# Mixture-of-experts loop with three resident weight sets, one extra block ahead of its loop, and four gather buffers

## The reference, cut to what matters

```python
D_MODEL, SEQ, CTX_LEN, N_EXPERTS, TOP_K, D_EXPERT = 1024, 256, 256, 32, 2, 512

# per layer, after the mixers
lg = h @ w_rg + b_rg                       # 4 groups, the best one is taken
le = (h @ w_re + b_re) of that group       # 8 experts, the best two are taken
weights = softmax(lg)[group] * top2_probabilities
for block in blocks_of_tokens_sorted_by_expert:
    ys = (silu(xb @ w_gate[e]) * (xb @ w_up[e])) @ w_down[e]
out = sum over the two experts of weight * ys      # back in token order
x = x + gate * out
...
return rms_norm(x, final_g)
```

## Time and profile before

| | us |
|---|---|
| median of 3 runs | 2103.83 (2101.32 to 2107.59) |
| the profiled execution, its own time | 2107.49 |
| its span, first to last instruction | 2105.7 |
| PE busy in it | 1875.1 (89%) |
| layer 0, first gate_up to the end of the last down | 637 to 1172 |
| layer 1, the same | 1565 to 2068 |

### The profile page before, as it was taken

How to read it: one execution, slowest core, us unless ns; L and a number is a source line. 1 busy time by engine, 2 the same in 40 slices (tenths; PEclk the granted TensorE clock), 3 DMA queues, 4 the chain that set the end, 5 groups by cost and what they waited for, 6 DMA issues and landing times.

```text
span 2105.7 us, 27927 instructions
## 1 busy us (share of the span) xinstructions
PE 1875.1 (89%) x9715; PEld 997.8 (47%) x9716; DVE 685.3 (33%) x1467; ACT 516.1 (25%) x1052; POOL 152.2 (7%) x190
## 2 busy tenths in 40 slices
PE   5799999999979999977999679989978989898985
PEld 2576666668743333322333367767943323232323
DVE  1456355445442111111111365574441111111112
ACT  2444444432231101100011254443220101110111
POOL 0035021000000000000000206130000000000000
PEclk8899999999989999988999799999989999999997
DMA  6446565223256999965999423233467989999992
GB/s 221 164 162 220 200 215 199 107 71 94 81 239 281 421 421 421 421 275 236 389 421 420 145 90 103 88 102 116 154 263 311 421 361 421 421 421 421 421 421 100
DMA packets 96042, 550.47 MB, mean 261 GB/s; under 512 B 14162, under 2 KB 15650, under 8 KB 42724
## 3 DMA queue, kind: packets, MB, share of 16 engines
q1 hardware_dynamic: 83108, 526.89, 63.1%
q0 software_dynamic: 4224, 11.35, 1.9%
q10 hardware_dynamic: 8640, 11.28, 1.5%
HBM read 537.15 MB, written 12.32 MB: 261 GB/s over the span
## 4 chain that ended last, share of the span: by engine, by line
PE 70%; DMA 12%; DVE 7%; ACT 5%; issue 3%; SPq 1%; ACTq 0%; DVEq 0%; POOL 0%; POOLq 0%
PE ps L724 17%; DMA moe<-in_w_exp_gate_up_dram 10%; PE ps L467 8%; PE ps L709 7%; PE ps L469 7%; PE ps L468 7%; PE ps L736 7%; PE ps L658 2%; PE ps L614 2%; PE ps L585 2%; PE ps L716 1%; PE ps L507 1%; PE ps L596 1%; DVE w_lo L1186 1%; PE ps L760 1%
## 5 line engine op out<-in xcount | busy, mean ns | idle before, releaser
L724 PE MATMUL ps<-moe,ht 128*64 128x512 f32 x2048 | 451.4, 593 | 22.8 <-DMA moe<-in_w_exp_gate_up_dram 22.8
L724 PEld LDWEIGHTS ps<-moe,ht 128*64 128x64 f32 x2048 | 150.2, 137 | 316.7 <-issue 291.6
L467 PE MATMUL ps<-ht_hi,w_hi 128*128 128x512 f32 (+1 forms) x736 | 268.6, 365 | 20.8 <-DVE ht_lo L1209 18.1
L468 PE MATMUL ps<-ht_lo,w_hi 128*128 128x512 f32 (+1 forms) x736 | 257.4, 350 | 0.0
L469 PE MATMUL ps<-ht_hi,w_lo 128*128 128x512 f32 (+1 forms) x736 | 257.3, 350 | 0.0
L1482 DVE TENSOR_TENSOR arena<-aux,ps 128x256 f32<-128x256 f32 x64 | 26.9, 421 | 687.9 <-ACT aux L1083 687.9
L736 PE MATMUL ps<-moe,arena 128*64 128x512 f32 x1024 | 231.4, 594 | 2.5 <-DVE arena L1503 2.5
L1186 DVE TENSOR_TENSOR w_lo<-ws,w_hi 128x1024 fp32r<-128x1024 f32 (+1 forms) x124 | 150.4, 1217 | 234.4 <-ACT w_hi L900 234.3
L709 PE MATMUL ps<-arena,ht 128*64 128x512 f32 x816 | 212.1, 630 | 4.7 <-DVE ht L1435 4.7
L467 PEld LDWEIGHTS ps<-ht_hi,w_hi 128*128 128x128 f32 x736 | 139.8, 190 | 70.9 <-issue 39.6
L900 ACT ACTIVATE w_hi<-ws 128x1024 fp32r<-128x1024 f32 (+1 forms) x124 | 127.4, 1027 | 187.5 <-PE ps L469 150.3
(11 more groups left out here) (220 smaller groups left out, 1984.6 us busy)
## 6 DMA issues: line engine op xcount, KB each, us to landing
moe<-in_w_exp_gate_up_dram SPq DMA_DIRECT2D x256, 1024.0 KB, 13.4
moe<-in_w_exp_down_dram SPq DMA_DIRECT2D x128, 1024.0 KB, 16.4
moe<-in_w_mod_dram SPq DMA_DIRECT2D x32, 1536.0 KB, 6.8
ws<-in_w_in_dram SPq DMA_DIRECT2D x92, 512.0 KB, 3.9
y_rows<-arena ACTq DMA_DIRECT2D x164, 64.0 KB, 5.6
ws<-in_w_branch_dram SPq DMA_DIRECT2D x16, 512.0 KB, 3.5
ws<-in_w_out_dram SPq DMA_DIRECT2D x16, 512.0 KB, 3.3
aux<-in_rpb_a_dram POOLq DMA_DIRECT2D x64, 64.0 KB, 3.1
```

The source lines that it names most:

```text
L467: pe.matmul(ps[:, bank, 0:cols], w[:, k, :], a_hi, start=(i == 0), stop=False)
L468: pe.matmul(ps[:, bank, 0:cols], w[:, k, :], a_lo, start=False, stop=False)
L724: mm = pe.matmul(ps[BLK * j:BLK * j + BLK, bank, :].rearrange("p (g n) -> p g n", g=2), x[:, at:at + BLK], w[:, k, 512 * j:512 * j + 512]. ...
```

## The change

It does three things in one edit.

1. **Three weight sets.** The third set lies in `ws` (24 KB, the slots of the mixers' weights), in `arena` (16 KB) and in `ht` (8 KB). For that, the routing scratch `r` moves from `arena` to `aux`, and the pairs of `xg`, `hid`, `hid_t`, `act_g`, `ysb`, of the PSUM banks of `gate_up` (2, 3) and `down` (4, 5), and the use of two `pick` buffers in the loop become one each. The loop has 10 passes of three bodies, and two experts follow behind it. SP asks for the weights of expert `e` when `turn_h`, then `down`, of expert `e - 3` are done; the last piece of the first third set waits for `hturn_done`, since it overwrites part of `ht`. SP waits at the end for `down` of expert 29, since the next layer's weights go into `ws`.
2. **The first extra block** stands outside the loop over extra blocks, which runs only if `n > BLK + MORE`.
3. **Four pairs of gather buffers**, so POOL's gathers wait for no tile.

```diff
-        xg = [part(ht_flat, 2 * i, 2) for i in range(2)]
-        hid = [part(arena, 34 + i, 1) for i in range(2)]
-        ysb = [part(arena, 40 + 2 * i, 2) for i in range(3)]
+        xg, xs = part(ht_flat, 0, 2), part(ht_flat, 2, 2)
+        hid, hid_t = part(arena, 34, 1), part(arena, 35, 1, 2, P)
+        ysb, ysb_o = part(arena, 40, 2), part(arena, 42, 1)
...
+        third = [part(ws_flat, 8 * i, 8, 2, D) for i in range(3)] + [part(arena, 24, 8, 2, D), part(arena, 16, 8, 2, D), part(ht_flat, 8, 8, 2, D)]
+        eights = [[part(moe, 48 * i + 8 * j, 8, 2, D) for j in range(6)] for i in range(2)] + [third]
...
+                load_expert(lambda w: w[l, 2], 2, range(5))
+                sp.wait_ge(g["hturn_done"].sem, g["hturn_done"].at(l, width(l) // P - 1, 1))
+                load_expert(lambda w: w[l, 2], 2, (5,))
...
+                    sp.wait_ge(g["hidt_done"].sem, NE * l + e - SLOTS + 1)
+                    load_expert(source, slot, range(4))
+                    sp.wait_ge(g["down_done"].sem, NE * l + e - SLOTS + 1)
+                    load_expert(source, slot, range(4, 6))
...
+                def expert(e, i, q):
+                    done, landed = NE * l + e, loads_before(l, q) + i + 1
+                    pe.wait_ge(g["xt_copied"].sem, xt0 + e + 1)
+                    pe.wait_ge(gu_in[q].sem, landed * 64)
+                    gate_up(2, xg, wgu[q])
...
+                    with pe.If(n > BLK):
+                        def more_block(b):
+                            more_slots(pe.snap(n_more, min_val=0, max_val=64), wgu[q], wd[q])
+                            pe.reg_add(n_more, n_more, 1)
+
+                        more_block(BLK // MORE)
+                        with pe.If(n > BLK + MORE):
+                            with pe.Fori(BLK // MORE + 1, w_all // MORE) as b:
+                                with pe.If(n > b * MORE):
+                                    more_block(b)
...
+                    pe.wait_ge(g["hidt_copied"].sem, done + 1)
+                    pe.wait_ge(g["y_copied"].sem, done + 1)
+                    down(4, hid_t, wd[q], g["down_done"].sem)
+
+                with pe.Fori(0, ROUNDS) as i:
+                    for q in range(SLOTS):
+                        expert(SLOTS * i + q, i, q)
+                for q in range(TAIL):
+                    expert(SLOTS * ROUNDS + q, ROUNDS, q)
...
-                    if tile >= 2:
-                        pool.wait_ge(g["comb"].sem, g["comb"].at(l, tile - 2))
```

More of the change, by code:

```diff
@@ L268, in hybrid_block, with loads_before @@
         bias_in = [g[f"bias{i}"] for i in range(4)]
[L269 to L273, removed]
+        gu_in, wd_in = [g[f"gu_in{i}"] for i in range(SLOTS)], [g[f"wd_in{i}"] for i in range(SLOTS)]
+        yg_got = [g[f"yg_got{i}"] for i in range(4)]
+        def loads_before(l, q):
+            return sum(len(range(q, NE, SLOTS)) for _ in range(l))
         def width(l):
@@ L781, in _ @@
                 pick_x(pick[1], range(nt))
[L782 to L790, removed]
-                        pe.nop(nofuse=True)
[L792 to L808, removed]
@@ L1068, in _ @@
                     act.reg_mov(n_more, 0)
[L1069 to L1071 removed]
+                    act.sem_inc(g["y_copied"].sem, 1)
+                    act.sem_inc(g["y_saved"].sem, 32)
                     act.sem_inc(g["yo_copied"].sem, 1)
@@ L1110, in _ @@
-                        with act.If(n > HALF):
-                            save_rows(ysb[s], act.snap(row + HALF, min_val=0, max_val=2 * NTOK), g["yt_saved"], first=HALF, rows=HALF)
-                            act.reg_add(n_tails, n_tails, 1)
-                        act.nop()
-                act.wait_ge(y_saved[0].sem, 32 * 16 * (l + 1) + 32)
-                act.wait_ge(y_saved[1].sem, 32 * 16 * (l + 1) + 32)
+                    act.nop()
+                    act.wait_ge(g["down_done"].sem, done + 1)
@@ new lines, in expert @@
+                    nc.scalar.activation(ysb, ps[:, 4, :], ACT.Copy).then_inc(g["y_copied"].sem, 1)
+                    act.wait_ge(g["y_copied"].sem, done + 2)
+                    act.wait_ge(g["yo_saved"].sem, act.snap(n_more, min_val=0, max_val=64) * 64 + 64)
+                    save_rows(ysb, row, g["y_saved"], rows=HALF)
+                    with act.If(n > HALF):
+                        save_rows(ysb, act.snap(row + HALF, min_val=0, max_val=2 * NTOK), g["yt_saved"], first=HALF, rows=HALF)
+                        act.reg_add(n_tails, n_tails, 1)
@@ L1116, in _ @@
+                    act.nop()
+                with act.Fori(0, ROUNDS) as i:
+                    for q in range(SLOTS):
+                        expert(SLOTS * i + q)
+                for q in range(TAIL):
+                    expert(SLOTS * ROUNDS + q)
+                act.wait_ge(g["y_saved"].sem, 32 * NE * (l + 1) + 32)
                 act.wait_ge(g["yt_saved"].sem, act.snap(n_tails, min_val=0, max_val=64) * 32 + 32)
@@ new lines, in expert @@
+                    dve.wait_ge(g["xt_done"].sem, xt0 + e + 2)
+                    copy_xg()
+                    dve.wait_ge(g["hidt_done"].sem, done + 1)
+                    v.tensor_copy(hid_t, ps[:, 1, 0:256].rearrange("p (c n) -> p c n", n=P)).then_inc(g["hidt_copied"].sem, 1)
+                    dve.wait_ge(g["xs_done"].sem, xs0 + e + 3)
+                    copy_xs()
+                    set_pick(pick[0], e + 3, 0, g["pick_set"])
+                with dve.Fori(0, ROUNDS) as i:
+                    for q in range(SLOTS):
+                        expert(SLOTS * i + q)
```

197 lines of the change are left out of this document (98 added, 99 removed).

## The result

The changed kernel takes 2359.04 us (median of 4 runs, 2352.91 to 2368.02) against 2104.93 (4 runs, 2101.32 to 2107.59): a ratio of 1.121, 95% interval 1.119 to 1.124. The forecast was 2062.5, in a range from 2054 to 2126. Both layers lose. From the first gate_up to the last down layer 0 now takes 691.7 us (635.16 to 1326.85) in place of 535.0 (636.91 to 1171.87), and layer 1 takes 595.2 (1717.57 to 2312.78) in place of 502.8 (1564.90 to 2067.70).

A forecast was written before the change was run, and what follows sets the result against it. Layer 0 was taken as limited by PE, layer 1 by transfers, extra blocks breaking both limits. Gains of 21.0 (layer 0), 19.4 (layer 1) and 0.9 (gather), 41.3 us, off 2103.83 gave 2062.5, range 2054 to 2126.

The forecast's parts named there:

- the empty turns: Layer 0, behind each extra block: PE's loop over further blocks turns and finds nothing; removing this was to gain 16.35 us.

The follow-up runs named there:

- e3: The kernel before, two slots, with its loop over extra blocks ended at the expert's own count, one copy of the block: 2074.48 us, ratio 0.986.
- e5: e3 with 110 never-run products per expert in PE's loop, layer 0's on 8 code blocks, layer 1's on 7: 2401.84 us, ratio 1.141.
- e6: The loops of e5 moved by never-run products ahead of them, layer 0's to 7 code blocks, layer 1's to 8: 2377.08 us, no ratio given.
- e1: The changed kernel with one copy of the extra block per expert, in a loop ending at the expert's own count: 2052.26 us, 0.975 of the kernel before.
- e7: e3 with PE's loop written out for eight experts per pass: 2124.75 us, ratio 1.010 to the kernel before.

## What to carry to other kernels

Count the instructions of a loop, the code that it jumps over included, and where it lies in blocks of 256: PE's loop stayed on up to 7 of them here, and on 8 or 9 it cost 10 to 20 us per pass of two or three experts. When code is copied to save a branch, look at the queue of instruction fetches in the trace: packets inside a loop that had none are the sign. A loop that ends at a run-time count saved the empty turns with no second copy at all (e3).

## What the runs showed of the hardware

- The place of a loop decides, not its length alone: a loop of 1726 instructions took 583 us on 7 code blocks and 822 on 8, one of 1633 took 504 and 734 (e5, e6).
- Code that never runs counts: e5 differs from e3 only in products that are jumped over, and its layer 0 takes 822 us in place of 509.
- A stall of 2 to 4 us costs more than itself: in the layers with many of them the granted clock is 0.86 to 0.95, right behind a stall of the changed kernel it was 0.63 (834.73 to 838.62), and its products took 81.5 us more in all than the same ones in e1.
- A jump over one extra block (262 instructions) was mostly free even in a loop that does not stay (e7, 19 of 32 experts of layer 0 at 15.0 or 15.1 us); one over two was not (the changed kernel, 2.6 us behind each gate_up of the pass shown).
